# Four transformer-like blocks on one core: the moving operand of every three-part fp32r product read from its last column to its first

## What is computed

```python
def sqrelu_mlp(h, w1, w2):
    return jnp.square(jax.nn.relu(h @ w1)) @ w2        # 1024 -> 4096 -> 1024
```

## Time and profile before

| | |
|---|---|
| median of 3 runs | 1960.39 us (1960.23 to 1961.43) |
| span of the profiled execution, from the first to the last instruction | 1959.2 us |
| TensorE busy | 1919.3 us, 98% of the span |
| TensorE weight load busy | 1607.6 us, 82% |
| DVE busy | 1400.5 us, 71% |
| ACT busy | 895.7 us, 46% |
| mean granted TensorE clock | 0.996 of full |
| DMA | 315.12 MB, 161 GB/s in the mean |

### The profile page before, as it was taken

How to read it: one execution, slowest core, us unless ns; L and a number is a source line. 1 busy time by engine, 2 the same in 40 slices (tenths; PEclk the granted TensorE clock), 3 DMA queues, 4 the chain that set the end, 5 groups by cost and what they waited for, 6 DMA issues and landing times.

```text
span 1959.2 us, 27475 instructions
## 1 busy us (share of the span) xinstructions
PE 1919.3 (98%) x10285; PEld 1607.6 (82%) x10285; DVE 1400.5 (71%) x2243; ACT 895.7 (46%) x1536; POOL 250.2 (13%) x332
## 2 busy tenths in 40 slices
PE   8999999999999999999999999999999999989998
PEld 4877788888888777889988888888888878878997
DVE  5898777888866655487997676767755567667765
ACT  3433355333343453576554224634233454557654
POOL 2101010211111200411101001101110021331000
PEclk9999999999999999999999999999999999999999
DMA  8434235655663451367875422655555245327763
GB/s 311 138 98 136 76 98 185 211 184 174 201 185 100 158 168 33 95 225 257 271 245 165 151 97 69 200 162 183 161 172 161 78 148 176 98 92 229 228 196 116
DMA packets 191827, 315.12 MB, mean 161 GB/s; under 512 B 14637, under 2 KB 114312, under 8 KB 191696
## 3 DMA queue, kind: packets, MB, share of 16 engines
q1 hardware_dynamic: 162512, 210.09, 33.0%
q0 software_dynamic: 29184, 103.29, 17.1%
HBM read 312.29 MB, written 1.05 MB: 160 GB/s over the span
## 4 chain that ended last, share of the span: by engine, by line
PE 82%; DVE 9%; issue 4%; ACT 2%; DMA 2%; POOL 1%; SPq 0%; DVEq 0%; POOLq 0%; ACTq 0%
PE bank L723 24%; PE bank L730 22%; PE bank L729 22%; PE bank L733 8%; DVE w L2242 3%; DVE acc L2267 2%; PE bank L728 2%; PE bank L726 2%; ACT junk L1642 1%; PE bank L785 1%; DMA raw<-in_mlp_w 1%; POOL st L3258 1%; PE bank L809 1%; DVE X L2386 1%; ACT w L1610 1%
## 5 line engine op out<-in xcount | busy, mean ns | idle before, releaser
L1610 ACT ACTIVATE w<-raw 128x1024 fp32r<-128x1024 f32 (+4 forms) x390 | 399.1, 1031 | 555.8 <-PE bank L730 481.8
L2242 DVE TENSOR_TENSOR w<-raw,w 128x1024 fp32r<-128x1024 f32 (+3 forms) x372 | 439.2, 1189 | 229.2 <-ACT w L1610 228.8
L723 PE MATMUL bank<-HH,w 128*128 128x256 f32 (+1 forms) x1552 | 509.5, 328 | 3.4 <-DVE HH L2369 2.0
L729 PE MATMUL bank<-HL,w 128*128 128x512 f32 (+1 forms) x1232 | 412.1, 334 | 0.0
L730 PE MATMUL bank<-HH,w 128*128 128x512 f32 (+1 forms) x1232 | 411.9, 334 | 0.0
L2267 DVE SCALAR_TENSOR_TENSOR acc<-ada,sc,acc 128x512 f32<-128x512 f32 x518 | 362.4, 746 | 2.3
L723 PEld LDWEIGHTS bank<-HH,w 128*128 128x128 f32 x1552 | 291.0, 188 | 30.5 <-issue 4.4
L723 PE MATMUL bank<-w,UH 128*128 128x512 f32 x768 | 300.7, 392 | 0.3 <-DVE UL L2544 0.3
L730 PE MATMUL bank<-w,UL 128*128 128x512 f32 x768 | 299.1, 390 | 0.0
L729 PE MATMUL bank<-w,UH 128*128 128x512 f32 x768 | 298.9, 389 | 0.0
L729 PEld LDWEIGHTS bank<-HL,w 128*128 128x128 f32 x1232 | 230.2, 187 | 26.1 <-issue 0.2
(11 more groups left out here) (354 smaller groups left out, 2610.1 us busy)
## 6 DMA issues: line engine op xcount, KB each, us to landing
raw<-in_mlp_w SPq DMA_DIRECT2D x256, 512.0 KB, 4.4
ada<-in_mod_w POOLq DMA_DIRECT2D x96, 512.0 KB, 4.5
ada<-in_ada_w POOLq DMA_DIRECT2D x80, 512.0 KB, 4.7
raw<-in_ml_w_qkvo SPq DMA_DIRECT2D x28, 512.0 KB, 3.7
raw<-in_conv_w_in SPq DMA_DIRECT2D x24, 512.0 KB, 4.2
raw<-in_ada_w SPq DMA_DIRECT2D x12, 512.0 KB, 6.1
raw<-in_mla_w_o SPq DMA_DIRECT2D x8, 512.0 KB, 3.9
raw<-in_gla_w_v SPq DMA_DIRECT2D x8, 512.0 KB, 4.0
```

The costliest lines, as they stand in the source:

```text
L723: pe.matmul(o, sh, mh, start=start, stop=False, skip_group_check=True)
L729: pe.matmul(o, sh, ml, start=False, stop=False, skip_group_check=True)
L1610: act.activation(k.halves(n)[0], k.raw[(NDIRECT + n) % NRAW][:, 0:m], ACT.Copy).then_inc(*k.w_hi.up("w hi", n))
L2242: dve.tensor_tensor(low, k.raw[(NDIRECT + n) % NRAW][:, 0:m], high.bitcast(F32), ALU.subtract).then_inc(*k.w_lo.up("w lo", n))
```

## The change

Inside `mm3`, the output and both moving operands are turned round in the free dimension before the three (or, with `late`, the other three) matmuls are issued. The first column that is read is the last one, and its result is written to the last place of the piece of the bank; the stationary operands, the number of matmuls, the waits and the signals are as before. What stands in the bank afterwards is the same.

```diff
     def mm3(o, st, mv, start, stop, late=None):
 
         sh, sl = st
-        mh, ml = mv
+        o, mh, ml = [x[:, ::-1] for x in (o, *mv)]
         pe.matmul(o, sh, mh, start=start, stop=False, skip_group_check=True)
         if late is not None:
 
```

## The result

The changed kernel takes 2003.21 us (2001.43 to 2005.09, four runs) against 1960.49 us before (four runs now, one more than in the table of before); the ratio is 1.0219, with a 95% interval from 1.0205 to 1.0234. It is 43 us slower. The profiled execution took 2005.09 us with a span of 2003.3 us, 44.1 us above the span before.

What follows compares the result with a forecast made beforehand. The prediction took TensorE's `mm3` matmuls to bound the kernel; 8640 matmuls x 0 added nothing to the 1959.2 us span, so the median, 1.2 us above, stayed at 1960.4 us. Range: 1946 to 1998 us.

Steps and rivals of the forecast that it cites:

- What bounds the kernel: Whole kernel: TensorE busy 98% of 1959.2 us, `mm3` 72% of the chain; matmul cost times number sets the time.
- The counts and the method: Matmuls of `mm3`: 8640 changed, 5472 with 512 columns, 2784 with 256; cost read as distance between starts, 0.2267 and 0.1156 us.
- Rate by column: Columns streaming within each `mm3` matmul: reading and writing downwards was taken to cost zero more per column.
- rival B: Fetch or write in each matmul: descending access runs at half the rate, 1415 us more, 3375 us; chance 0.10.
- the reversed scan: VectorE's scan at line 2932, 256 elements, takes 0.67 us forward and reversed; taken as sign that descending access costs nothing more.
- The fixed part: Time per matmul in which no column moves, 13.4 ns (9 ns at 256 columns); claimed unchanged by the new start address.
- Rival A: Beginning of each matmul: a descending start costs 4.6 ns (2.7 ns at 256 columns), 34 us more, 1994 us; chance 0.20.
- the disturbed rows: Matmuls after four transposes at 378.91 us, out of rhythm: 0.231 us each with 512 columns, 0.118 with 256.
- Rival C: Start of each matmul: a descending start shrinks the columnless time; 25 us less, 1935 us, at best 1888 us; chance 0.10.
- Rival D: Lowering of the program: both ends turned back to ascending order, nothing changes, 1960.4 us; chance 0.05, inside "same".

## Why the prediction was wrong

- **What bounds the kernel** held. TensorE's products set the time; 46 to 49 us more of them became 44 us of span; the remainder came out of waits, which the shift of the chain from VectorE to TensorE fits.
- **The counts and the method** held: 8640 matmuls, 5472 and 2784 of them in the forms that matter, and the distance of the starts as the quantity to watch. The 128-column form kept its pace (0.112 us), which fits the reading that the load sets it; no run tests that reading.
- **Rate by column, nothing.** Right in its outcome: the 512 columns don't run at half the rate (rival B). But the argument from the reversed scan carried no weight. What does halve the rate is a step of 2.
- **The fixed part, "I take no change".** This is the step that failed. Its size was 6.6 ns for 512 columns and 4.4 for 256, in place of 0. The reason given was that an accumulation keeps its distance and the weight load is untouched. The first held: the bank's side costs nothing in either direction (ratio 1.0001). The loads stayed the same instructions. But neither reason covers the fetch of the moving operand, which is where the time went (ratio 1.0206 with the fetch alone turned). The part isn't fixed: 11 of its 13.4 ns go when the moving operand stays at one place. Upwards it hangs on the places of both streams, downwards it is 233.3 ns in all at 59 of 64 stationary places.
- **Rival A** named the right place, a start-to-start distance longer in every wide matmul, and was priced at 1994 us by the disturbed rows, 4.6 and 2.7 ns. (The 2.7 is a rounding: the six distances take 0.702 us in the trace, so it should be 1.4, and A's own price 1990 us.) The measured 6.6 and 4.4, less what came out of waits, make 2003 us, above the range's upper end of 1998. The disturbed rows were read as a passing loss of rhythm that settles. They were better evidence than the forecast took them for, since they show that the distance isn't a constant of the array. It was also in the code: `NARROW_AT = 2` and the pads behind the weight buffers, which let `w` begin at the same remainder by 256 bytes as `HH` and `UH`, serve nothing but a place, and the prediction didn't ask what they are for.
- **Rival C** is excluded for 512 columns, but not for direction in general: with 256 columns and no shift a downward read was the faster one, 118.3 against 120.0 ns.
- **Rival D**, a change that lowers to the same program, is out: the distances moved in the whole kernel, and turning the fetch alone moved them as well.

What is shown is that the downward fetch of the moving operand costs the time, and how much. What stays open is why a fetch that moves takes 11 ns more than one at a fixed place, why only an upward one finds 226.7, and whether the downward one loses a good place or pays a price of its own: the two whole-kernel prices that don't add up speak for the first, the 4.5 ns that remain with 256 columns and the load at one place for the second. The mirror test, in which the stationary operand is turned as well, wasn't tried.

## What to carry to other kernels

A kernel whose operands have been laid out with care may owe some per cent to where they begin. A change of order that leaves counts, bytes and waits alone can lose that, and shifting an operand by 32 bytes can lose it as well. Before calling a reordering free, read the distance between starts, look for pads and offsets that serve nothing else, and measure a row of the bare instructions in both orders. A good place found that way has to be measured again in the kernel, where the same places gave two rhythms.

## What the runs showed of the hardware

- An fp32r matmul of 512 columns at the full clock takes 215.8 ns from start to start when its moving operand stays at one place, 226.7 at the best places and up to 240.0 at the worst seen.
- A descending write into a bank costs nothing (ratio 1.0001). A descending fetch of 512 columns costs 6.6 ns against the best placed ascending one; from the same place the difference was between -1.7 ns (stationary operand at 7: 233.3 after 235.0) and 11.2 (moving operand at 3: 240.0 after 228.8).
- A step of 2 in the moving operand halves the rate (0.453 us for 512 columns).
- The place of the *stationary* operand changes the distance of upward reads too, by up to 8 ns with 512 columns (226.7 to 235.0) and by 10 with 256 in one kernel (113.3 to 123.3; 126.7 once in another). Downwards with 512 columns 59 of 64 places give 233.3.
- The same places can give two rhythms: with `NARROW_AT = 16` whole rows of 256-column products ran at 113 ns and others at 118.
